# Handing the store of the convolution's transposition from GpSimd's queue to SyncE's, with four row loads on each, and a second centring ahead of the reciprocal

## What is computed

```python
def layer_norm(x, g, b):
    mu = jnp.mean(x32, axis=-1, keepdims=True)
    xc = x32 - mu
    y = xc * lax.rsqrt(jnp.mean(xc * xc, axis=-1, keepdims=True) + RMS_EPS)
    return (y * g + b).astype(x.dtype)

def conformer_conv(x, w_in, b_in, conv_w, conv_b, ln_g, ln_b, w_out, b_out):
    a, g = jnp.split(x @ w_in + b_in, 2, axis=-1)
    h = a * jax.nn.sigmoid(g)
    h = lax.conv_general_dilated(h, ...31 taps, depthwise, causal...) + conv_b
    h = jax.nn.silu(layer_norm(h, ln_g, ln_b))
    return h @ w_out + b_out
```

## Time and profile before

| | |
|---|---|
| median of 3 runs | 2165.45 us (2162.18 to 2166.38) |
| the profiled execution's own time | 2165.45 us |
| its span | 2163.6 us |
| mean granted TensorE clock | 0.961 of full |
| TensorE busy | 1975.9 us (91%) |
| VectorE busy | 1603.9 us (74%) |
| ScalarE busy | 1054.5 us (49%) |
| GpSimd busy | 554.2 us (26%) |

### The profile page before, as it was taken

One profiled execution on the slowest core, in us unless ns is written; L12 is line 12 of the kernel. 1 busy time (PEld: TensorE's weight loads), 2 busy tenths in 40 slices (PEclk: granted clock), 3 DMA queues, 4 the chain that ended last, 5 costly groups with the idle time before them and its releaser, 6 DMA issues. The chain is left out here.

```text
span 2163.6 us, 30090 instructions
## 1 busy us (share of the span) xinstructions
PE 1975.9 (91%) x11159; PEld 1064.6 (49%) x11159; DVE 1603.9 (74%) x1699; ACT 1054.5 (49%) x1395; POOL 554.2 (26%) x347
## 2 busy tenths in 40 slices
PE   7988988889399999999994989948899999999999
PEld 5775446644244455444543455533444444444444
DVE  6855637743789999999987463483696898889876
ACT  5333326722378888888865463482332223323320
POOL 2121130000123333333320010012022564656440
PEclk9999999999599999999997999969999999999999
DMA  6111420051289999999986464437101211111111
GB/s 238 40 40 40 123 43 1 1 214 52 104 350 410 415 410 408 397 403 401 393 343 237 164 212 145 135 127 250 39 1 40 75 42 58 58 66 50 58 58 78
DMA packets 81067, 363.69 MB, mean 168 GB/s; under 512 B 13968, under 2 KB 28048, under 8 KB 48400
## 3 DMA queue, kind: packets, MB, share of 16 engines
q1 hardware_dynamic: 62384, 309.97, 36.7%
q0 software_dynamic: 18592, 52.47, 7.2%
HBM read 337.21 MB, written 37.75 MB: 173 GB/s over the span
## 5 line engine op out<-in xcount | busy, mean ns | idle before, releaser
L432 PE MATMUL ps<-split,xt 128*128 128x512 f16 (+1 forms) x848 | 319.3, 377 | 32.1 <-DMA xt<-z_rows 26.4
L434 PE MATMUL ps<-split,xt 128*128 128x512 f16 (+1 forms) x848 | 319.3, 376 | 0.0
L433 PE MATMUL ps<-split,xt 128*128 128x512 f16 (+1 forms) x848 | 319.2, 376 | 0.0
L649 DVE SCALAR_TENSOR_TENSOR split<-stage,split 128x2048 f16<-128x2048 f32 x128 | 289.6, 2284 | 5.6 <-ACT split L645 3.8
L645 ACT ACTIVATE split<-stage 128x2048 f16<-128x2048 f32 x128 | 240.5, 1904 | 94.1 <-PE ps L434 94.1
L1358 POOL TENSOR_TENSOR stage<-stage 128x1024 f32<-128x1024 f32 x52 | 145.2, 2792 | 259.1 <-DVE split L834 256.1
L432 PE MATMUL ps<-xt,split 128*128 128x512 f16 (+1 forms) x528 | 191.4, 362 | 9.8 <-issue 8.2
L433 PE MATMUL ps<-xt,split 128*128 128x512 f16 (+1 forms) x528 | 191.3, 362 | 0.0
L434 PE MATMUL ps<-xt,split 128*128 128x512 f16 (+1 forms) x528 | 190.9, 362 | 0.0
L649 DVE SCALAR_TENSOR_TENSOR arena<-arena 128x2048 f16<-128x2048 f32 x64 | 146.3, 2286 | 3.1 <-ACT arena L645 3.1
L432 PEld LDWEIGHTS ps<-split,xt 128*128 128x128 f16 x848 | 83.6, 99 | 125.5 <-issue 29.3
(11 more groups left out here) (525 smaller groups left out, 4750.4 us busy)
## 6 DMA issues: line engine op xcount, KB each, us to landing
stage<-in_w_gate SPq DMA_DIRECT2D x64, 1024.0 KB, 7.3
stage<-in_w_up SPq DMA_DIRECT2D x64, 1024.0 KB, 7.5
arena<-in_w_down SPq DMA_DIRECT2D x64, 1024.0 KB, 7.8
stage<-in_w_mlp SPq DMA_DIRECT2D x32, 1024.0 KB, 4.9
arena<-in_conv_taps POOLq DMA_DIRECT2D x32, 640.0 KB, 5.0
stage<-in_w_dense_a SPq DMA_DIRECT2D x16, 1024.0 KB, 8.4
stage<-in_w_dense_b SPq DMA_DIRECT2D x12, 1024.0 KB, 9.6
resid<-in_x SPq DMA_DIRECT2D x16, 512.0 KB, 4.7
```

Source lines behind the costliest of these rows:

```text
L432: nc.tensor.matmul(out_ap, lh, rh, start=start, stop=False)
L433: nc.tensor.matmul(out_ap, lh, rl, start=False, stop=False)
L434: return nc.tensor.matmul(out_ap, ll, rh, start=False, stop=stop)
L649: nc.vector.scalar_tensor_tensor(out=wlo(s), in0=wstage(s), scalar=WS, in1=whi(s), op0=ALU.mult, op1=ALU.subtract).then_inc(s_wo[s], 1)
```

## The change

The store of each tile to `z_rows[k]` goes from GpSimd to SyncE and counts on `s_rb[k]`, the semaphore of SyncE's row loads. SyncE waits for the tile's low half, stores, waits for the landing, loads phases 0 to 3 and then issues the x2 load. GpSimd waits for the same landing and loads phases 4 to 7. TensorE's wait is adapted to the counts. On VectorE `centre(1)` is put ahead of the reciprocal; after the scale of k only `centre(k + 2)` follows. The amount of computation and the bytes moved are the same.

```diff
@@ SyncE @@
             for k in range(KT):
-                sp.wait_ge(s_zp[k % 2], 16 * 4 * (k // 2) + 16)
-                rows_back(sp, k, range(5), s_rb[k])
+                sp.wait_ge(s_cl, k + 1)
+                sp.dma_start(z_rows[k], ZN[:, k, :, :].rearrange("p a x -> p (a x)")).then_inc(s_rb[k], 16)
+                sp.wait_ge(s_rb[k], 16 * (PH + 2))
+                rows_back(sp, k, range(4), s_rb[k])
                 sp.dma_start(H[:, k, :], x2_phase[k]).then_inc(s_x[k], 16)
@@ GpSimd @@
             for k in range(KT):
-                pool.wait_ge(s_cl, k + 1)
+                pool.wait_ge(s_rb[k], 16 * (PH + 2))
                 if k >= 2:
                     pool.wait_ge(s_zp[k % 2], 16 * 4 * (k // 2))
-                pool.dma_start(z_rows[k], ZN[:, k, :, :].rearrange("p a x -> p (a x)")).then_inc(s_zp[k % 2], 16)
-                pool.wait_ge(s_zp[k % 2], 16 * 4 * (k // 2) + 16)
-                rows_back(pool, k, range(5, PH), s_zp[k % 2])
+                rows_back(pool, k, range(4, PH), s_zp[k % 2])
@@ VectorE @@
-            centred = [centre(0)]
+            centred = [centre(0), centre(1)]
...
-                    for n in {0: (1, 2), KT - 2: (), KT - 1: ()}.get(k, (k + 2,)):
-                        centred.append(centre(n))
+                    if k + 2 < KT:
+                        centred.append(centre(k + 2))
@@ TensorE @@
-                pe.wait_ge(s_rb[k], 16 * (PH + 1 + 5))
+                pe.wait_ge(s_rb[k], 16 * (PH + 2 + 4))
```

## The result

| | before | after |
|---|---|---|
| median | 2165.91 us (2162.18 to 2168.10) | 2185.24 us (2181.62 to 2187.34) |
| runs | 4 | 4 |
| span of the profiled execution | 2163.6 us | 2183.9 us |

The ratio is 1.0089, 95% interval 1.0067 to 1.0111: slower by 0.9%, 19.3 us between the medians and 20.3 us between the profiled spans. The direction is the one forecast. The size is not: 6.9 us were forecast, with 2180 us as the upper end of the range.

A forecast was written before the change was run, and what follows sets the result against it. TensorE's waits were put down to the chain of trips through DRAM. 1445.5 + 7 x 7.8 + 5.2, then 5.18 for block 7 and 0.9 for the clock, gave +6.9 us: 2172.3 us, range 2161 to 2180 us.

The forecast's parts named there:

- x2 load, issue to landing: SyncE's 512 KB load, issued ahead of the next store: taken to land in 4.0 us, bounds 3.7 and 5.3.
- store behind the x2 load's landing: On SyncE's queue the store doesn't overtake the x2 load and lands 1.3 us after it.
- period: One store-and-load-back trip per tile: 2.5 us row loads, 4.0 x2 landing, 1.3 store, so 7.8 us against 6.86 before.
- row loads to block 7: From the start of the last tile's row loads to TensorE's start of block 7: 5.2 us.
- low clock in block 7: After idling, TensorE's clock falls to half, a loss of 1.7 us; half of it, 0.9 us, charged to block 7.
- end of the stage moves by: End of the convolution stage on TensorE: 1511.4 against 1504.46, +6.9 us, all reaching the program's end.
- The first tile and the first store: Before the loop: low half 1.0 us late, store landing in 2.8 us, row loads from 1445.5 against 1444.90, +0.6 us.
- the case that led to it: More contention: x2's landing stays at 5.3 us as eight row loads run into it; period 9.1 us, 2181.5 us; chance 0.08.
- rivals on overlap: Partial overlap: the store shares with x2 and lands 3.8 us from its issue; period 7.1 us, 2167.5 us; chance 0.23.
- a store that isn't held up: SyncE's queue takes load and store at once, the store lands as if alone; period about 6.0 us, 2158.9 us; chance 0.12.
- Landing to TensorE: From the row loads' start to TensorE's block: 5.2 us against 7.7 before, a gain of 2.5 us taken once.
- What was to be hidden: Gains' load and first MLP weights, queued on SyncE, issued some 4 us later at no cost; first use over 50 us later.

The follow-up runs named there:

- e2: Kernel before with four row loads on each queue, the store still on GpSimd: 2181.2 us, ratio 1.0076.
- e3: Kernel before with the store moved to SyncE alone, five and three row loads and the old centring kept: 2183.2 us, ratio 1.0086.
- e9: Changed kernel with each x2 load reading 128 neighbouring rows where it read every eighth: 2185.4 us, ratio 1.0088.
- e14: Changed kernel with the x2 load issued ahead of SyncE's four row loads, the next store still behind it: 2173.2 us, ratio 1.0033.
- e8: Changed kernel with each row load cut to 16 target partitions and all eight phases, same bytes: 2181.2 us, ratio 1.0069.
- e4: Changed kernel with SyncE issuing the next tile's store ahead of the x2 load: 2162.8 us, ratio 0.9991.
- e15: Changed kernel with the x2 loads after the loop and a second 512 KB store in their place: 2170.4 us, ratio 1.0029.

## Why the prediction was wrong

Read in the profiled execution, against the terms of the sum:

| step | forecast | measured |
|---|---|---|
| first row loads start | 1445.5 | 1445.93, of which 0.57 us from before the loop |
| x2 load, issue to landing | 4.0 us | 6.0 us median |
| store behind the x2 load's landing | 1.3 us | 1.2 us (k = 0: 1448.42 + 5.9, store seen at 1455.57) |
| period | 7.8 us | 9.56 us |
| seven periods | 54.6 us | 66.95 us |
| row loads to block 7 | 5.2 us | 5.67 us |
| low clock in block 7 | 0.9 us | 1.7 us (6.88 - 5.18) |
| end of the stage moves by | 6.9 us | 20.97 us, 20.4 without the 0.57 |

Of the 13.5 us that were missed (20.4 - 6.9), 12.3 are seven times the error in the period, 0.5 the way from the row loads to block 7 and 0.8 the clock. The direction was right for the reason given, a longer chain of trips; the term below was far too small.

- **The first tile and the first store** came as worked out: the low half starts at 1442.00, with the 0.57 us off at 1441.43 against 1441.4, and the store lands in 2.6 us.
- **The step that failed is the x2 load's landing**, "I take 4.0 us, close to 3.7 because no store runs beside it now". The 3.7 us was of k = 7 in the kernel before, with no store near it; only loads, of the gains and weights, followed. In the changed kernel a store of 512 KB follows 0.5 us behind on the same queue, so one does run beside it. Its own k = 7, with none, lands in 4.6 us, the others in 6.0, and it is the same in e2, e3 and e9: 4.7, 4.2 and 4.4 us at k = 7 against medians of 6.6, 5.7 and 6.0. e14 shows that 3.7 us holds for a load whose way is free. I had the upper bound of 5.3 us in the text, and gave the case that led to it 0.08; it was the nearest, and even 5.3 was too low, since in the earlier trace rows the stores came ahead of the loads in every turn but k = 2, whose x2 load landed in 5.0 us, and no row had both on one queue.
- **That the store lands 1.3 us behind x2** was right, and the earlier trace rows read rightly. The rivals on overlap and on a store that isn't held up are out.
- **The mechanism as I told it was too narrow.** I wrote of a chain on one queue. e2 has two queues and loses some 15 us of the 19. What both halves of the change do is let x2 be issued ahead of the store. Before, five and three loads put the store 1.06 us ahead of x2 in the first turn; nobody would see a dependence there, for none is written down. The turn k = 2 of the kernel before, in the trace that I had, showed what losing that order costs, and would have given the period nearly: 9.45 us against the measured 9.56, though 1.3 us of its length were GpSimd's pause.
- **Landing to TensorE** was a gain of 2.0 us and not 2.5 (5.67 against 7.7 us).
- **The low clock** took its full 1.7 us from block 7. I had charged half without a row that said so.
- **What was to be hidden was hidden**: nothing in the profile after shows the later gains or MLP weights to be waited for.

Not settled is why one or two engines end late when x2 and the store follow each other behind the row loads. Its being a load and its place were shown to matter, the slow first microsecond belongs to the load in either place, and neither the stride of its rows (e9) nor the way the row loads are cut (e8) removed the loss. What holds the late engines up, and why a load starts at a low rate, was not found.

## What to carry to other kernels

In a serial trip, store, wait, load back, look at what else is issued between one wait and the next store, on every queue, and put what nobody waits for behind the store: half a microsecond of issue order was worth 22 us here (e4 against the changed kernel). Splitting loads more evenly over two queues moves the issue times of everything behind them, and this can turn an order that no semaphore keeps. Look at single turns too and not only at their mean: one turn of the kernel before showed the loss beforehand. Better still, give each store a semaphore of its own and issue it one tile ahead, so that its landing leaves the chain. And a landing time is worth only as much as the traffic behind and beside the row it comes from: take it from a row with the same neighbours, or let the range go to the worst one seen.

## What the runs showed of the hardware that was not expected

- The same 512 KB load lands in 3.7 us ahead of four row loads, in 4.6 us (a single load, k = 7) directly behind them with only loads following, and in 6.0 us behind them with a 512 KB store following.
- A store on GpSimd's queue is held up as much by a load issued 0.13 us ahead of it on SyncE's queue (6.6 us) as a store on SyncE's own queue (6.65 us).
- At the start of a 512 KB load the DMA engines were 92% occupied at 163 GB/s, and 97% at 353 GB/s a moment later; ahead of all row loads (e14) it was 98% at 127 GB/s, then 99% at 392. A store began at 383 GB/s (e15). Their busy share is not their rate.
- At equal size, a load in that place adds 3.19 us to a turn and a store 1.24 us, each with 0.5 us of issue.
